# A decoder step on one core: cached keys gathered in smaller pieces and in pairs, new keys scored inside the prompt attention

## The reference

```python
def mla_attend(q_lat, q_rope, ckv, krope, q_pos, k_pos):
    s = jnp.einsum('bthc,blc->bhtl', ql, ckv) + jnp.einsum('bthr,blr->bhtl', qr, krope)
    s = jnp.where(qp[:, None] >= k_pos[None, :], s * scale, -1e30)
    p = jax.nn.softmax(s, axis=-1)
    return jnp.einsum('bhtl,blc->bthc', p, ckv)

past_ckv = cache_ckv[l, page_table].reshape(bs, past_len, KV_LORA)     # 128 values a position
past_kr = cache_krope[l, page_table].reshape(bs, past_len, QK_ROPE)    # 32 values a position
keys_ckv = jnp.concatenate([past_ckv, ckv], axis=1)
```

## Time and profile before

| What | Before |
|---|---|
| median of 3 runs (lowest, highest) | 1874.95 us (1874.04, 1878.89) |
| the profiled execution | 1874.86 us, its span 1873.1 us |
| PE busy, matmuls | 1718.2 us, 92% of the span, 11012 records |
| DVE, ACT, POOL busy | 831.0, 403.5, 274.4 us |
| PE over the span, mean granted clock | 0.945 |
| PE idle before L1125 (scores over the cache) | 35.9 us, of it 22.8 us until DVE's key transposes |
| DVE idle before key transposes, until a gather | 28.6 us |

### The profile page before, as it was taken

The page is one execution under the profiler, slowest core; times in us unless marked ns, Lnnn a source line. Parts: engine busy times, 40 slices in busy tenths (PEclk is TensorE's granted clock), DMA queues, the critical chain, the costliest instruction groups (busy, mean ns, idle before and its releaser), DMA issues. The chain is left out here.

```text
span 1873.1 us, 26847 instructions
## 1 busy us (share of the span) xinstructions
PE 1718.2 (92%) x11012; PEld 1145.7 (61%) x11012; DVE 831.0 (44%) x1652; ACT 403.5 (22%) x839; POOL 274.4 (15%) x279
## 2 busy tenths in 40 slices
PE   8998977999999999999899998889999999899980
PEld 6876645888887463333378765468888864533330
DVE  4676865433333351111539678553333324511117
ACT  0125512111111121111310364121111111211111
POOL 0002010000000002364000110200000005123625
PEclk9998978999999989999999989789999999899995
DMA  9104133332231667995750320442222235799974
GB/s 278 64 24 159 51 140 120 124 90 63 84 107 68 272 249 298 416 413 208 244 158 1 126 87 24 176 147 79 70 88 88 86 127 236 278 380 413 417 275 160
DMA packets 136092, 322.56 MB, mean 172 GB/s; under 512 B 33582, under 2 KB 95780, under 8 KB 113380
## 3 DMA queue, kind: packets, MB, share of 16 engines
q1 hardware_dynamic: 103270, 204.45, 30.6%
q0 software_dynamic: 31200, 114.61, 16.1%
q10 hardware_dynamic: 1502, 1.80, 0.3%
HBM read 360.20 MB, written 29.48 MB: 208 GB/s over the span
## 5 line engine op out<-in xcount | busy, mean ns | idle before, releaser
L1239 PE MATMUL ps<-space 128*128 128x272 f32 x1024 | 250.3, 392 | 0.0
L1724 PE MATMUL ps<-space,xT 128*64 128x512 f32 x864 | 226.7, 595 | 0.0
L468 PE MATMUL ps<-xT,space 128*128 128x272 f32 (+1 forms) x960 | 224.1, 397 | 1.4 <-DMA space<-in_w_in 1.4
L1239 PEld LDWEIGHTS ps<-space 128*128 128x128 f32 x1024 | 194.6, 190 | 40.1
L468 PEld LDWEIGHTS ps<-xT,space 128*128 128x128 f32 (+1 forms) x960 | 182.9, 191 | 42.2 <-DMA space<-in_w_in 1.8
L1247 PE MATMUL ps<-space 128*128 128x272 f32 x640 | 157.1, 392 | 0.0
L1985 DVE SCALAR_TENSOR_TENSOR space<-space,ps 128x256 f32<-128x256 f32 x32 | 21.5, 672 | 265.0 <-ACT space L1826 253.5
L1247 PEld LDWEIGHTS ps<-space 128*128 128x128 f32 x640 | 121.6, 190 | 25.1
L1239 PE MATMUL ps<-xT,space 128*128 128x272 f32 x512 | 127.8, 393 | 0.0
L1724 PEld LDWEIGHTS ps<-space,xT 128*64 128x64 f32 x864 | 69.7, 137 | 90.7 <-issue 88.3
L1125 PE MATMUL ps<-space,fifth 32*32 32x256 f32 x2560 | 92.1, 500 | 35.9 <-DVE space L882 22.8
(11 more groups left out here) (389 smaller groups left out, 2201.6 us busy)
## 6 DMA issues: line engine op xcount, KB each, us to landing
space<-in_w_in SPq DMA_DIRECT2D x44, 1024.0 KB, 5.5
space<-in_exp_w_down SPq DMA_DIRECT2D x32, 1024.0 KB, 12.4
space<-in_exp_w_gate SPq DMA_DIRECT2D x30, 1024.0 KB, 10.2
space<-in_exp_w_up SPq DMA_DIRECT2D x30, 1024.0 KB, 12.2
space<-in_w_o SPq DMA_DIRECT2D x8, 1024.0 KB, 6.5
space<-x_rows SPq DMA_DIRECT2D x16, 512.0 KB, 6.0
space<-y_rows SPq DMA_DIRECT2D x16, 512.0 KB, 7.2
space<-in_p_attn SPq DMA_DIRECT2D x8, 512.0 KB, 6.4
```

The source lines that it names most:

```text
L468: t = nc.tensor.matmul(ps[0:m, 2 * (n % 4) + h, 0:HN], w[:, f, c * P:c * P + m], k.xT[:, f, h, :], start=(f == 0), stop=(f == KD - 1))
L1239: t = m.matmul(out, w[:, f, :], x[:, f, :], start=(first and f == 0), stop=(f == H - 1), skip_group_check=True)
L1724: i = m.matmul(ps[r, 6 + t % 2, :], k.xgT[:, t % 2, f, r], gate_up_of(g)[:, f], start=(f == 0), stop=(f == KD - 1), skip_group_check=True)
```

## The change

Four things change, in both layers.

1. **The new keys** are scored at the head of turn 6 (`FRESH`), in the upper half of PSUM bank 0, which the 256-wide scores of turns 4 to 7 leave free. DVE's mask, sum, maximum and negative go into turn 6, ACT's two exponentials behind those of turn 8. The last block of the prompt is copied by ACT instead of DVE.
2. **The first half's keys** are gathered in 16 pieces of 128 rows of 1024 floats (0.5 MB), a piece for one step of one sequence. Step 0's four go out at the start, steps 1 and 2's eight behind the projections, each awaited, step 3's first two behind the output transfers and the fourth rotary gather, its last two behind the last values of the prompt.
3. **The second half's keys** stay at 1 MB a gather, but go out in pairs: pair j (j = 0 to 3) waits for the values of step j and for the scores of step j + 2. Pairs 0 and 1 serve steps 4 and 5, pairs 2 and 3 serve steps 6 and 7. The second half's rotary gathers wait for the scores of step 1. A third buffer `krT` lets DVE transpose rotary keys a step earlier.
4. **SP** fills two branches' weights behind the values of step 5, instead of one there and the next in `merge`.

```diff
+def cached(k, s, b):
+    place, at = (2 * s + b // 2, b % 2) if s < LOADS else (4 * ((s - LOADS) // 2) + b, s % 2)
+    return place, k.ckv[place][:, 1024 * at:1024 * at + 1024]
...
@@ gpsimd
-            for u in range(4, AHEAD):
-                load_keys(k, pool, u)
-                pool.wait_ge(*due(k, k.c_in[u], 16))
+            for s in range(1, LOADS - 1):
+                for b in range(4):
+                    load_keys(k, pool, s, b)
+                    pool.wait_ge(*due(k, k.c_in[2 * s + b // 2], 16 * (b % 2 + 1)))
             pool.wait_ge(*due(k, k.s_out, 16 * (3 + 3 * DB + 8 + 4)))
             load_rotary(k, pool, 0, 3)
-            load_keys(k, pool, KEEP - 2)
+            for b in range(2):
+                load_keys(k, pool, LOADS - 1, b)
             pool.wait_ge(*due(k, k.c_v, TURNS))
-            load_keys(k, pool, KEEP - 1)
-            pool.wait_ge(*due(k, k.d_kr, 4 * LOADS))
-            for b in range(4):
-                load_rotary(k, pool, 1, b)
-            for u in range(KEEP, WIDE):
-                pool.wait_ge(*due(k, k.d_pv, 4 * (u // 4 - 1)))
-                load_keys(k, pool, u)
+            for b in range(2, 4):
+                load_keys(k, pool, LOADS - 1, b)
+            for s in range(LOADS):
+                if s == 0:
+                    pool.wait_ge(*due(k, k.d_kr, 4 * LOADS))
+                    pool.wait_ge(*due(k, k.d_s, 2))
+                    for b in range(4):
+                        load_rotary(k, pool, 1, b)
+                pool.wait_ge(*due(k, k.d_pv, 2 * s + 2))
+                pool.wait_ge(*due(k, k.d_s, s + 3))
+                for e in range(2):
+                    load_wide(k, pool, 2 * s + e)
...
@@ sync
             sp.wait_ge(*due(k, k.d_pv, 2 * (STEPS - 3) + 2))
-            fill_branch(k, l, sp, 0, 0)
+            sp.wait_ge(*due(k, k.d_kr, 4 * STEPS))
+            for b in range(2):
+                fill_branch(k, l, sp, 0, b)
...
@@ vector, the steps
                 if u == 0:
-                    dve.wait_ge(*due(k, k.d_pvn, 1))
-                    v.tensor_copy(k.outs[:].rearrange("p h n -> p (h n)"), ps[:, V, 0:2 * P]).then_inc(k.d_o, 1)
+                    dve.wait_ge(*due(k, k.d_pnt, 1))
+                    v.tensor_copy(k.pnT[0:HS].rearrange("p h n -> p (h n)"), ps[0:HS, MISC, 2 * P:4 * P]).then_inc(k.d_pnc, 1)
...
+                for s in range(2 if u == 0 else u + 3, min(u + 4, STEPS)):
+                    for b in range(4):
+                        turn_rotary(s, b)
                 if u + 2 < STEPS:
-                    for b in range(4):
-                        turn_rotary(u + 2, b)
...
@@ tensor, the turns
             for i in range(TURNS + 3):
+                if i == FRESH:
+                    new_scores()
+                if i == FRESH + 2:
+                    pe.wait_ge(*due(k, k.d_m, 2))
...
-                if i == TURNS:
-                    new_scores()
```

114 lines of the change are left out of this document (61 added, 53 removed).

## The result

| | before | changed |
|---|---|---|
| median | 1876.52 us (1868.60 to 1882.38, 16 runs) | 1883.64 us (1879.17 to 1889.31, 16 runs) |
| ratio | | 1.0037, 95% interval 1.0027 to 1.0047 |
| profiled execution | 1874.86 us, span 1873.1 us, mean granted clock 0.945 | 1883.33 us, span 1881.5 us, clock 0.938 |

The change made the kernel slower by 7 us, and the interval excludes no change. The forecast was 1873.7 us, a hair faster. The miss is 9.9 us; the range (1864 to 1884) just held the time.

A forecast was written before the change was run, and what follows sets the result against it. PE, busy for 92% of the span, was taken to bound the kernel. The terms 5.5 - 4.4 + 2.2 - 3.4 - 0.8 - 2.7 + 1.4 + 1.0 gave -1.2 us, so 1873.7 us; range 1864 to 1884.

The forecast's parts named there:

- A: Turn 6 of the prompt attention: 17 small matmuls move later turns back 2.76 us in both layers, +5.5 us.
- F: End of pass 2 to start of pass 4: four gathers in a row become two pairs, -2.7 us.
- E: End of pass 1 to end of pass 2: second half's rotary gathers go out at pass 1's end, -0.8 us.
- H: Behind step 5's values: loading two branches' weights instead of one may lengthen a PE gap, +1.0 us.
- B: End of the prompt turns: new-key matmuls taken out, so pass 0 starts earlier, -4.4 us.
- D: End of pass 0 to start of pass 1: DVE's reduction starts at once, -1.7 us per layer, -3.4 us.
- G: End of pass 4 to start of pass 6: the same plan of paired gathers, +1.4 us.
- C: Beside pass 0: two gathers of 0.5 MB instead of one of 1 MB, +2.2 us.
- The third: Before turn 12: first half's fourth rotary gather comes too late, PE loses 10 us per layer, 1894 us; chance 0.05.
- The second: Value steps behind passes 2 and 4: a pair starves PE as long as four gathers, +9.6 us, 1883.3 us; chance 0.13.
- The first: Passes 3 and 5: the clock holds, so they may run at 3.3 us; sum -8.2, 1866.7 us; chance 0.29.
- The fourth: Passes 3 and 5 stay slow for a reason that stays, +8.5 us per layer, 1890.7 us; chance 0.03.

The follow-up runs named there:

- e2_turn6: The kernel before with one part of the change alone, the new keys scored in turn 6: 1876.63 us, ratio 1.0004.
- h2_before_again: The kernel before, nothing altered, run again on another kind of chip than the first: 1855.80 us, ratio 0.9999.
- h3: The changed kernel without the wait for the scores of step s+2 at the pairs of steps 4 and 5 alone: 1858.54 us, ratio 1.0022.
- h4: The changed kernel without the wait for the scores of step s+2 at the pairs of steps 6 and 7 alone: 1863.66 us, ratio 1.0048.
- E5: Not a run: the moment when pass 5, PE's 160 score records of cache step 5, ends.
- E0: Not a run: the moment when pass 0, PE's 160 score records of cache step 0, ends.
- e1_end: The changed kernel with the new keys scored behind the last turn again, gathers and fills as changed: 1892.66 us, ratio 1.0104.
- e4_nogate: The changed kernel with all second-half pairs waiting for the values of step s alone, not the scores of step s+2: 1865.07 us, ratio 0.9957.
- g4_changed_again: The changed kernel, nothing altered, run again on another kind of chip than the first: 1873.44 us, ratio 1.0095.
- e3_turn10: The changed kernel with the new keys scored in turn 10 instead of turn 6: 1886.38 us, ratio 1.0048.

## Why the prediction was wrong

**Two terms of the sum failed, A and F.** In the profiled executions the attention missed its forecast by 5.6 us: A by 5.8 and F by 3.2, against smaller errors the other way in E and H. The other 4.0 us lie outside the attention, where the prediction put nothing.

**Term A was mis-sized by half: 11.3 us for 5.5.** The forecast held the small matmuls against the time that they took at the full clock, and even its bound, +8, counted only them. At the lower level they took 3.7 us a layer, and turns 6 and 7 stayed at that level as well. The trace of the kernel before had this: turn 6 began at 189.59 us in layer 0 with the clock going up only at 189.75, and at 1110.99 us in layer 1 with the clock going up only at 1114.76. The window that I took for turn 6 starts at 1112.00 and averages over that. For the whole part (A, B, D) the forecast was -2.3 us; e2_turn6 measured +1.6, so it makes 3.9 of the 9.9 us. It didn't decide the sign: e2_turn6 stands at 1.0004.

**Term F came out at +0.5 us for -2.7, and it holds the dependency that made the kernel slower.** Pass 4 needs a pair that is asked for only behind pass 3. I wrote that down, and let the passes freed of starvation pay for it. On the first chip the chain had nearly its forecast length: the pairs were taken up by DVE 9.0 to 9.5 us behind their issue where I had 8.7, and S4 came at E3 + 11.3 and 11.2 us where I had 10.4. But the order puts pass 3 on that chain. Its 4.6 us became 7.7 in layer 0, with the hole of 2.90 us in it, and there F lost 2.8 us; in layer 1 pass 3 took 3.38 us and F won 2.3 us, 1.8 forecast. In the kernel before, a slow pass 3 cost nothing in h2_before_again: 9.05 or 3.61 us, E2 to S4 was the same. On the first chip step 4 waited for its burst as well, and started 16.2 and 17.0 us behind its first issue, so the starvation that I counted as won was mostly hidden behind that wait. What the dependency costs is shown by taking it out: the same kernel is 15 us faster on one chip (18.6 by the medians) and, h3 and h4 in sum, 22 us on others. These figures say why the changed kernel is slow; they are not terms of my sum.

**G was right by luck.** +1.7 for +1.4 us is made of -0.4 in layer 0, where pass 5 took 3.39 us, and +2.1 in layer 1, where it took 6.23 us with a hole of 2.26 us; S6 came at E5 + 11.6 and 11.1 us and not 10.4.

**B, C and D hold.** Turn 8 to S0 gave -4.6 us for -4.4; pass 0 with two gathers 5.24 us for the 5.3 implied; S1 lies 4.35 us behind E0 for 4.4.

**E holds on the first chip and turns round on the others.** I wrote that DVE's rotary transposes wait for these gathers and that the reader comes later still. The reader does; but the key transposes of pass 3 and the reduction of step 2 stand behind them. On the first chip the starved value step put pass 2 off to 253.73 us, and the pass ran at the lower clock until 259.3 us; that covered the wait. Where pass 2 took 3.6 us, pass 3 started 9.3 us behind E2. I had named the queue and not followed it to its end.

**H cost nothing** that could be told apart: the hole in the last value step was 1.59 us, 1.31 before, and that stretch of the attention became shorter.

**The rivals.** The third, the late rotary gather, was real: in e1_end, where turn 11 is not delayed, it cost 7 and 9.5 us a layer. The pieces took 4.5 us each where I estimated 4.0. That it did not happen in the changed kernel was luck: with turn 6 longer by my 2.76 us, DVE would have wanted the gather at 209.5 us, and in e1_end it had it at 211.37; only the mis-sized A made room for it. The second (a pair starves PE as a burst does, in the value steps) did not happen in its place: S3 and S5 came 4.2 to 5.0 us behind E, not 7.6. Single holes came instead inside pass 3 of layer 0 and pass 5 of layer 1. The first (the clock holds) showed in pass 5 of layer 0 and pass 3 of layer 1, 3.39 and 3.38 us. The fourth, by which passes 3 and 5 stay slow, fell: all four took 3.4 to 7.7 us for its 9.4 and 8.3. The rule of the Trainium skill that I had kept for it (SBUF — State Buffer, section Who interferes with whom) does not describe PE's time on the first chip, where passes 3 and 5 beside four gathers took 8.2 to 9.5 us; it does describe the pass 3 of 3.61 us beside four gathers in h2_before_again.

**What the holes are.** In the holes of 2.90 and 2.87 us (266.87 and 296.33 us of the changed kernel) the trace has one packet of 16 KB on the queue of kind "instruction", at 267.55 and 297.00 us; by that of 2.26 us (1218.56) one starts at 1218.39. A hole of 3.98 us in pass 3 of layer 0 of h2_before_again has one at 257.54 us, with the gathers at 97% of the DMA engines' time. So PE may stand still because its next instructions come late behind the gathers' data. This is a coincidence in the traces, not shown by a run: other such packets beside gathers have no hole.

**What stays open.** The attention accounts for 4.4 of the 8.4 us between the two profiled spans. Of the rest 2.0 us came between the attentions and 2.5 behind the second, with 0.5 won ahead of the first. The changed kernel's execution had a stretch of 3.4 us at the lower clock at the start of the merge (331.3 us), none there before, and 6.8 us more of them in layer 1 behind the attention. Neither e2_turn6 nor e4_nogate has these, nor has g4_changed_again the one at the merge; I found no cause. Between h2_before_again and g4_changed_again the attention accounts for 14.5 of 16.7 us. That the two kinds of chip differ in how pass 2 is held up is shown (8.8 and 3.38 us with the same gathers), why is not. Why E1 to S4 took 3.7 us longer in layer 1 of e3_turn10 than in the changed kernel wasn't settled.

## What to carry to other kernels

When a change delays requests so as to keep them off the engine that is busy, price the delayed request as a chain: its issue, its landing, the consumers in the queue behind it. The saving in stalls was 7 us and the chain cost 20 (e4_nogate). And ask first whether the stall that you save is on the path: a pass 3 of 9.05 or 3.61 us left step 4 where it was (h2_before_again).

Undo the parts of a change one by one before blaming the largest difference in the profile. Here the largest local difference (turn 6) was harmless, and it hid a flaw in another part.

A transpose taken up early on an in-order engine is only free if its data are there; if not, all that stands behind it waits.

## What the runs showed of the hardware

- With 17 small matmuls of 16 columns in turn 6, where the clock was at 0.50, it rose to 1.00 later: at 198.16 us and not 189.75, with one arrangement of gathers as with the other (e2_turn6 stayed at 0.50 from turn 4 to turn 8). In turn 10, at 1.00, they left the clock where it was in layer 0 and cost 2.8 us; in layer 1 it fell for 3.4 us behind them.
- The same program on other chips starves differently: pass 2 of the kernel before, 8.8 us on the first chip and 3.38 us on another; its pass 3, 9.5 us in both layers on the first and 9.05 and 3.61 us on the other; with a total of 1875 and 1856 us. A change that trades starvation for waits therefore has another value on each: 1.0037 and 1.0095. That the chips' starvation is the reason for the two ratios is argued from the stretches, not isolated.
- Awaited gathers of 0.5 MB, issued one by one, took 4.5 us each from issue to issue (4.3 to 5.0); DVE had the second of a pair of 1 MB gathers 9.0 to 9.5 us behind the first issue.
- While gathers' data flowed, PE stood still for 2.2 to 4.0 us at a time, with no releaser in the profile, beside a 16 KB packet on the queue of kind "instruction" (holes of 2.90, 2.87, 2.26, 3.98 and 2.23 us).
